# A transformer trunk layer on one Trainium2 core: all of x loaded first, and part of the modulation vector made by TensorE with the weight chunk stationary

## The reference, cut to what matters here

```python
c_act = silu(c)                                   # c: (1, 1024)
mod = c_act @ w_ada + b_ada                       # w_ada: (1024, 6144)
sh_m, sc_m, g_m, sh_f, sc_f, g_f = split(mod, 6)  # each 1024 wide
u = layer_norm(x) * (1 + sc_m) + sh_m             # x: (1024, 1024)
z = u @ w_in
...                                               # pooling, attention, convolution, merge, MLP
```

## Time and profile before

| | |
|---|---|
| runs | 1427.02, 1428.12, 1428.88 us; median 1428.12 |
| profiled execution, its own time | 1426.88 us |
| its span (first to last instruction) | 1425.1 us |
| PE busy | 1393.0 us (98%) |
| DVE busy | 969.4 us (68%) |
| ACT busy | 647.3 us (45%) |
| POOL busy | 421.8 us (30%) |
| mean granted TensorE clock | 0.993 |

### The profile page before, as it was taken

One profiled execution on the slowest core, in us unless ns is written; L12 is line 12 of the kernel. 1 busy time (PEld: TensorE's weight loads), 2 busy tenths in 40 slices (PEclk: granted clock), 3 DMA queues, 4 the chain that ended last, 5 costly groups with the idle time before them and its releaser, 6 DMA issues.

```text
span 1425.1 us, 17299 instructions
## 1 busy us (share of the span) xinstructions
PE 1393.0 (98%) x6522; PEld 1148.6 (81%) x6522; DVE 969.4 (68%) x1340; ACT 647.3 (45%) x914; POOL 421.8 (30%) x453
## 2 busy tenths in 40 slices
PE   7799999999999999999999999999999999999996
PEld 3688888888888888888888888888888888888885
DVE  5789677776479946464768797556565646437787
ACT  5522677777542124101616774443345535343251
POOL 1006465555566000000024327333444200001315
PEclk9899999999999999999999999999999999999998
DMA  9775465654565232762622555444445878456361
GB/s 347 266 266 159 148 185 156 188 168 149 161 234 172 89 104 79 245 192 86 200 114 89 183 181 193 142 145 146 156 163 207 297 277 299 162 211 236 118 222 60
DMA packets 159083, 256.42 MB, mean 180 GB/s; under 512 B 11352, under 2 KB 81422, under 8 KB 159000
## 3 DMA queue, kind: packets, MB, share of 16 engines
q1 hardware_dynamic: 144152, 204.97, 43.1%
q0 software_dynamic: 14848, 50.34, 10.5%
HBM read 182.36 MB, written 68.71 MB: 176 GB/s over the span
## 4 chain that ended last, share of the span: by engine, by line
PE 91%; DVE 5%; ACT 2%; issue 1%; DMA 1%; SPq 0%; DVEq 0%; ACTq 0%
PE ps L2065 24%; PE ps L2067 24%; PE ps L2066 24%; PE ps L2214 11%; PE ps L2254 2%; PE ps L2264 2%; PE ps L2279 2%; PE ps L2085 1%; DVE part_lo L1922 1%; PE ps L2129 1%; PE ps L2404 1%; DVE q L1983 0%; DMA k_raw<-tw_scratch 0%; DMA ada<-in_w_ada_dram 0%; DVE w_lo L1387 0%
## 5 line engine op out<-in xcount | busy, mean ns | idle before, releaser
L2065 PE MATMUL ps<-act_hi,w_hi 128*128 128x512 f32 (+1 forms) x480 | 187.2, 390 | 9.4 <-DVE act_lo L1482 9.4
L1922 DVE TENSOR_TENSOR part_lo<-k_raw,part_hi 128x1024 fp32r<-128x1024 f32 x112 | 146.1, 1332 | 58.6 <-ACT part_hi L935 55.4
L2067 PE MATMUL ps<-act_hi,w_lo 128*128 128x512 f32 (+1 forms) x480 | 184.6, 385 | 0.0
L2066 PE MATMUL ps<-act_lo,w_hi 128*128 128x512 f32 (+1 forms) x480 | 184.6, 385 | 0.0
L2065 PE MATMUL ps<-part_hi 128*128 128x512 f32 x448 | 174.3, 389 | 0.0
L2066 PE MATMUL ps<-part_lo,part_hi 128*128 128x512 f32 x448 | 174.3, 389 | 0.0
L2067 PE MATMUL ps<-part_hi,part_lo 128*128 128x512 f32 x448 | 174.3, 389 | 0.0
L935 ACT ACTIVATE part_hi<-k_raw 128x1024 fp32r<-128x1024 f32 x112 | 116.4, 1059 | 113.6 <-DMA k_raw<-tw_scratch 48.8
L2065 PEld LDWEIGHTS ps<-act_hi,w_hi 128*128 128x128 f32 x480 | 91.1, 190 | 28.4 <-issue 5.9
L1387 DVE TENSOR_TENSOR w_lo<-w_raw,w_hi 128x1024 fp32r<-128x1024 f32 x51 | 65.9, 1291 | 65.6 <-ACT w_hi L935 65.6
L2066 PEld LDWEIGHTS ps<-act_lo,w_hi 128*128 128x128 f32 x480 | 91.2, 190 | 18.4 <-issue 1.0
(11 more groups left out here) (260 smaller groups left out, 3202.4 us busy)
## 6 DMA issues: line engine op xcount, KB each, us to landing
k_raw<-h_scratch SPq DMA_DIRECT2D x112, 256.0 KB, 4.2
w_raw<-in_w_in_dram SPq DMA_DIRECT2D x42, 512.0 KB, 4.1
ada<-in_w_ada_dram SPq DMA_DIRECT2D x8, 2048.0 KB, 9.6
tw_rows<-in_w_ff_dram POOLq DMA_DIRECT2D x64, 256.0 KB, 4.1
tw_scratch<-tw_sum POOLq DMA_DIRECT2D x32, 512.0 KB, 3.7
h_scratch<-h_sum POOLq DMA_DIRECT2D x64, 256.0 KB, 3.0
k_raw<-tw_scratch SPq DMA_DIRECT2D x64, 256.0 KB, 5.4
pair_raw<-in_w_ff_dram SPq DMA_DIRECT2D x13, 1024.0 KB, 6.3
```

What stands on the lines that cost most here:

```text
L1922: nc.vector.tensor_tensor(part_lo[s][:, :, :], k_raw[rs][:, :, :], f(part_hi[s][:, :, :]), ALU.subtract)\
L2065: nc.tensor.matmul(out, sh, mh, start=first, stop=False)
L2066: nc.tensor.matmul(out, sh, ml, start=False, stop=False)
L2067: return nc.tensor.matmul(out, sl, mh, start=False, stop=last)
```

## The change

SP loads c, then all eight x tiles, then chunk 0, the small rows, chunk 2, weight blocks 0 and 1, chunk 1, weight block 2, chunk 3. Norm and transpose go tile by tile in place of pairs. Chunk 0, chunk 2 and the first half (k = 0 to 3) of chunk 3 are made by TensorE with the chunk stationary: for each of four groups of 128 columns and each k, one product whose stationary operand is 128x128 of the chunk and whose moving operand is one column of `c_act`. They give columns at once, so `save_ada_row` and `row_columns` go. The two halves of a sum lie in separate PSUM columns and are added by VectorE. VectorE makes chunk 1 whole and the second half of chunk 3.

```diff
@@ SP
             def load_ada(i):
-                if i == 3:
-                    sp.wait_ge(head_ps_done, 1)
+                if i in (3, 5):
+                    sp.wait_ge(reduced, DIRECT_ORDER.index(i - 3) + 1)
                 elif i == 4:
                     sp.wait_ge(partial_done, 1)
-                elif i == 5:
-                    sp.wait_ge(head_ps_done, 4)
                 elif i == 6:
-                    sp.wait_ge(partial_done, 2)
+                    sp.wait_ge(reduced, 4)
...
-            load_ada_half(0, 0)
-            load_x(range(2))
-            load_ada_half(0, 1)
-            load_x(range(2, 4))
+            load_x(range(ST))
+            load_ada(0)
...
-            load_ada_half(2, 0)
-            load_x(range(4, 6))
-            load_ada_half(2, 1)
-            load_x(range(6, ST))
+            load_ada(2)
             load_block(0)
+            load_block(1)
             load_ada(1)
-            load_block(1)
+            load_block(2)
             load_ada(3)
-            load_block(2)
@@ ACT
-            for i in range(0, ST, 2):
+            for i in range(ST):
                 take_root(i, i)
-                take_root(i + 1, i + 1)
-                norm(i, i, mid[:, i, :])
...
+                if i >= 1:
+                    norm(i - 1, i - 1, mid[:, i - 1, :])
+                if i >= 2:
+                    save_tile(i - 2)
+            cut_hi(0)
@@ DVE
+            for t in range(ST):
+                dve.wait_ge(x_in[t], 16)
+                stats(mid[:, t, :], t)
+                if t >= 1:
+                    scale_bias(t - 1, t - 1)
+            scale_bias(ST - 1, ST - 1)
...
             def start_chunk(i):
-                dve.wait_ge(ada_in[i % 3], 16 * (i // 3 + 1))
+                if i == 3:
+                    dve.wait_ge(ada_end_in[0], 32)
+                else:
+                    dve.wait_ge(ada_in[i % 3], 16 * (i // 3 + 1))
...
+                k0 = 4 if i == 3 else 0
...
             def mixer_columns(h):
...
-                link(nc.vector.tensor_tensor(out, total, bias, ALU.add))
+                link(nc.vector.tensor_tensor(out, low, bias, ALU.add))
                 scale = mod[:, KT + 4 * h:KT + 4 * h + 4]
+                if h == 0:
+                    link(nc.vector.tensor_tensor(out, high, out, ALU.add))
+                else:
+                    link(nc.vector.tensor_tensor(scale, ps[:, 7, 28:32], scale, ALU.add))
                 nc.vector.tensor_scalar_add(scale, scale, 1.0).then_inc(mod_done, 1)
...
+            for t in (ST - 2, ST - 1):
+                dve.wait_ge(z_done, t + 1)
+                dve.wait_ge(x_copied, ST - 2)
+                nc.vector.tensor_copy(x_t[:, :, t * P:(t + 1) * P], tile_banks(t)).then_inc(x_copied, 1)
...
             mixer_columns(0)
-            dve.wait_ge(z_done, ST)
-            nc.vector.tensor_copy(x_t[:, :, (ST - 1) * P:ST * P], tile_banks(ST - 1)).then_inc(x_copied, 1)
             cut_lo(0)
             cut_u_lo(0)
             cut_u_lo(1)
             cut_lo(1)
             cut_u_lo(2)
+            cut_u_lo(3)
             start_chunk(1)
-            cut_u_lo(3)
+            cut_lo(2)
             end_chunk(1)
-            cut_lo(2)
             ada_chunk(3)
             mixer_columns(1)
@@ PE
+            def direct_chunk(i, half):
+                pe.wait_ge((ada_in, ada_end_in)[half][i % 3], 16 * (i // 3 + 1))
+                if i == 3:
+                    pe.wait_ge(cols_done, 1)
+                for m in range(4):
+                    for k in range(4 * half, 4 * half + 4):
+                        col = 16 * half + 4 * i + m
+                        ins = nc.tensor.matmul(ps[:, 6 + i % 2, col:col + 1], ada[i % 3][:, k, m * P:(m + 1) * P],
+                                               c_act[:, k:k + 1], start=k % 4 == 0, stop=k % 4 == 3)
                 return ins
...
+            for i in range(6):
+                transpose_x(i)
             pe.wait_ge(head_sb_done, 2)
-            row_chunk(0, 0)
-            transpose_x(0)
-            transpose_x(1)
-            row_chunk(0, 1).then_inc(head_ps_done, 1)
-            transpose_x(2)
-            transpose_x(3)
+            direct_chunk(0, 0)
+            transpose_x(6)
+            direct_chunk(0, 1).then_inc(reduced, 1)
+            transpose_x(7)
...
-            row_chunk(2, 0)
-            transpose_x(4)
-            row_columns(0)
-            transpose_x(5)
-            row_chunk(2, 1).then_inc(head_ps_done, 1)
-            transpose_x(6)
-            row_columns(2)
-            transpose_x(7)
+            direct_chunk(2, 0)
+            direct_chunk(2, 1).then_inc(reduced, 1)
...
             for n in range(2):
                 for k in range(2, 4):
                     rows_part(n, k)
+            direct_chunk(3, 0)
             pe.wait_ge(w_lo_done, 3)
             for k in range(4):
                 rows_part(2, k)
-            row_columns(1)
-            row_columns(3)
+            reduce_first(1)
+            reduce_first(3)
```

More of the change, by code:

```diff
@@ L66 @@
 N_DIRECT = 2
-ROW_ORDER = (0, 2, 1, 3)
-ADA_BANKS = {0: 0, 2: 1}
+DIRECT_ORDER = (0, 2, 1, 3)
 P1_BANKS = (4, 2, 0, 6, 0, 2)
@@ L125, in trunk_layer @@
     h_pad = at("h_pad", [P, 2, PAD + SEQ], f32, X + 84 * KB)
-    ada_row = [h_pad[0:1, i // 2, PAD + i % 2 * HALF:PAD + (i % 2 + 1) * HALF] for i in range(4)]
     z_pool = mid[:, 0:2, :]
@@ L960, in _ @@
             nc.scalar.activation(c_sig[:, :], c_raw[:, :], ACT.Sigmoid).then_inc(head_sb_done, 1)
-            def save_ada_row(i):
-                act.wait_ge(head_ps_done, {0: 1, 2: 4}[i])
-                copy(ada_row[i], ps[0:1, ADA_BANKS[i], :]).then_inc(head_sb_done, 1)
             def save_tile(i):
@@ L1434, in start_chunk @@
                     dve.wait_ge(reduced, i - 3)
-                link(nc.vector.tensor_scalar(partial_of(i)[:, :], ada[i % 3][:, 0, :], c_act[:, 0:1], None, ALU.mult))
-                add_rows(i, range(1, 4))
+                k0 = 4 if i == 3 else 0
+                link(nc.vector.tensor_scalar(partial_of(i)[:, :], ada[i % 3][:, k0, :], c_act[:, k0:k0 + 1], None,
+                                             ALU.mult))
+                add_rows(i, range(k0 + 1, 4))
             def end_chunk(i):
-                if i in (1, 3):
-                    dve.wait_ge(ada_end_in[i % 3], 16 * (i // 3 + 1))
-                add_rows(i, range(4, 8))
+                if i == 1:
+                    dve.wait_ge(ada_end_in[1], 16)
+                add_rows(i, range(5 if i == 3 else 4, 8))
             def add_rows(i, ks):
@@ L1469, in mixer_columns @@
                 ks = slice(4 * h, 4 * h + 4)
-                out, total, bias = (t.rearrange("p (g k) -> p g k", g=2)[:, :, ks]
-                                    for t in (mod[:, 0:16], ps[:, 6 + h, 0:16], cols[:, 0:16]))
-                link(nc.vector.tensor_tensor(out, total, bias, ALU.add))
+                out, low, high, bias = (t.rearrange("p (g k) -> p g k", g=2)[:, :, ks] for t in (
+                    mod[:, 0:16], ps[:, 6 + h, 0:16], ps[:, 6 + h, 16:32], cols[:, 0:16]))
+                link(nc.vector.tensor_tensor(out, low, bias, ALU.add))
                 scale = mod[:, KT + 4 * h:KT + 4 * h + 4]
+                if h == 0:
+                    link(nc.vector.tensor_tensor(out, high, out, ALU.add))
+                else:
+                    link(nc.vector.tensor_tensor(scale, ps[:, 7, 28:32], scale, ALU.add))
                 nc.vector.tensor_scalar_add(scale, scale, 1.0).then_inc(mod_done, 1)
@@ L1483, in cut_u_lo @@
                     .then_inc(u_lo_done, 1)
+            for t in (ST - 2, ST - 1):
+                dve.wait_ge(z_done, t + 1)
+                dve.wait_ge(x_copied, ST - 2)
+                nc.vector.tensor_copy(x_t[:, :, t * P:(t + 1) * P], tile_banks(t)).then_inc(x_copied, 1)
+            dve.wait_ge(head_ps_done, 2)
+            nc.vector.tensor_copy(cols[:, 0:ROWS_A], ps[:, 7, PIECE:PIECE + ROWS_A])
+            nc.vector.tensor_copy(cols[:, ROWS_A:ROWS_A + ROWS_C], ps[:, 7, PIECE + P:PIECE + P + ROWS_C])\
+                .then_inc(cols_done, 1)
             mixer_columns(0)
-            dve.wait_ge(z_done, ST)
-            nc.vector.tensor_copy(x_t[:, :, (ST - 1) * P:ST * P], tile_banks(ST - 1)).then_inc(x_copied, 1)
             cut_lo(0)
@@ L2079, in _, with reduce_first @@
             pe.wait_ge(consts_done, 2)
[L2081 to L2086, removed]
-                return ins
[L2089 to L2095, removed]
-                for m in range(4):
[L2097 to L2101, removed]
+            def direct_chunk(i, half):
[7 more added lines that the diff above has]
+                                               c_act[:, k:k + 1], start=k % 4 == 0, stop=k % 4 == 3)
+                return ins
+            def reduce_first(i):
+                pe.wait_ge(partial_done, 1 + i // 2)
+                pe.wait_ge(cols_done, 1)
+                for m in range(4):
+                    col = (4 if i == 1 else 28) + m
```

(2 more changed lines are left out.)

## The result

The changed kernel takes 1446.0 us (median of four, 1445.01 to 1449.26) against 1428.1 before: ratio 1.013, 95% interval 1.0112 to 1.0147. The profiled execution took 1445.01 us with a span of 1443.2, so 18.1 more than the profiled one before. The median is inside the stated range (1432 to 1453), but 7.7 us above the forecast of 1438.3, and what fills those 7.7 us is the mechanism of rival A, in part.

What follows compares the result with a forecast made beforehand. TensorE (PE), busy 98% of the span, was taken as the bound, so head losses pass to the end: +7.2 + 3.4 - 0.6 + 0.2 = +10.2 us, forecast 1438.3 us; own range 1433 to 1442, stated range 1432 to 1453.

Steps and rivals of the forecast that it cites:

- rival A: Chunk products of stage one: PE stays at 1.2 GHz through all of them; sum +23.6 us, 1451.7 us; chance 0.2.
- The bound: Whole kernel: PE is busy 98% of the span; the head's gain or loss passes to the end one for one.
- Prices: One-column chunk products: 0.106 us a record, 3.4 us a half chunk, cost as before; small columns saved, 2.0 us.
- rival B: Chunk products: the weight loads hide under other products; put at -4 us, 1424 us; chance 0.07.
- Step 1: Head, x loaded first: ScalarE sets the pace, 2.4 us a tile; TensorE transposes tile 5 until 23.4 us.
- Step 3: Start of the chunk products: first 4 us at half speed, costing 2.1 us more; stage one ends at 42.2 us.
- sign of being wrong: Stretch of the chunk products: a clock of 0.50 throughout would show the forecast wrong.
- Steps 4 and 5: Modulation starts at 43.0 us, +7.2; stage two: half of chunk 3 +3.4, stall gone -0.6, third small operation +0.2.
- Step 6: SP's queue, block 2 ahead of chunk 3: DMAs idle some 9 us, slack 5 us or more, costs nothing.

## Why the prediction was right and where it was off

**The bound.** Right. What the head lost, +18.1 us by k = 4, is what the span lost.

**Prices.** Right at full clock: 0.107 us a record, 3.72 us for the first half chunk with its tail. The weight loads did not hide: rival B is out.

**Step 1.** ScalarE sets the pace, but 2.13 us a tile and not 2.4 (norms at 15.15, 17.32, 19.45), since its operations overlap by 0.1 each; and x tile 0 was there at 5.0, not 5.8. Tile 5 was done at 21.7 in place of 24.0, 2.3 us to the good.

**Step 3 failed.** "I take it to be still at 1.2 GHz when the chunk products begin [...] the first 4 us of products run at half speed." It was the other way round. By their lengths the transposes ran at full speed from 18.6 us on, the first half chunk too, and then the clock fell and stayed down to the end of the chunk products. The stretch from tile 5 to the last product of chunk 2 took 28.2 us and not 18.2: +10.0, less the 2.3 of step 1, is the 7.7 by which the forecast was short. The term was the clock's: 2.1 us in the forecast, 12.1 by the trace (28.2 less the 16.1 of the same work at full clock). Rival A had the cause right and was too high by 5.7 us (1451.7 for 1446.0), because tile 5 was done 2.3 us earlier and the first half chunk ran at full clock, 3.3. The sign of being wrong that the prediction gave, a clock of 0.50 throughout, came true in all but the first quarter of the products. The forecast's own range, 1433 to 1442, missed; the time lies in the stated range since that takes in A's value. Rival A had a chance of 0.2; the trace of before held no row against it but one stretch of a microsecond behind full products, and I should have given it about half. What I used against it, 59 to 60 us in the earlier trace rows, was too short a stretch and stood behind full products: the half chunk at 67.40, behind such products too, also ran at 1.00, and in four other profiles the clock fell just behind it.

**Steps 4 and 5.** Modulation starts 0.7 us after the last product (50.56), as worked out. Stage two grew by 3.1 us (2.8 expected: the half chunk 3.5, the stall at 48.86 gone, a longer stretch at half speed). VectorE ended chunk 3 at 70.5, six microseconds before TensorE took it, as said. The run with chunk 3 on VectorE gave back 2.9.

**Step 6.** Right: nothing, by the run that exchanges the two loads. The DMAs stood idle (0 GB/s from 36 to 49 us), for some 17 us and not 9, since the low part of block 0, which releases block 2, came 7.6 us later than forecast (51.7 for 44.1).

Of the 18 us, by the runs: undone alone, the one-column form of chunks 0 and 2 brings 8 to 9 and the half of chunk 3 on TensorE some 3. Undone together they bring 16.4 (1446.0 less 1429.6), so 4 to 5 us come only with both; 2 to 3 us are left for the loads, the pace and the order, the late start among them. Where the shared part lies: with both undone TensorE reaches the columns of chunk 1 18.5 us after its first product of block 0 (61.01 less 42.48), with the form alone undone after 23.5. The half of chunk 3 is 3.5 of that difference and the dip behind it about 1.5, which the profile of the changed kernel did not have; the half-speed stretches behind the gaps, which differ by 1 to 2 us between kernels, and the attention stage hold the rest. How these share it was not told apart.

## What to carry to other kernels

A matrix-vector product with the matrix stationary and one column moving cost about what the other form did while the clock was up (3.7 us a half chunk for 3.6), but a long row of them ran at half the clock (6.8), and so did the transposes between. Price such a row at both clocks, and if it must be, let more columns move: 64 equal ones cost nothing here and gave 9 us. They are no surety: one run of ten with them took 1445.58 us, at a lower clock. And before work is taken off one engine and put on another, ask which of the two ends last in that stage after the move: here 3.1 us off VectorE were worth nothing and 3.5 us on TensorE cost 2.9.

## What the runs showed of the hardware that I had not expected

TensorE's clock fell from 2.4 to 1.2 GHz while the engine was busy in every microsecond, under products of one moving column (clock 0.50 from 27 to 33 and 36 to 49 us), and stayed at 2.4 GHz under the same products with 64 columns moving (31 to 38 us). The Trainium skill (TensorE: Matmul & The Clock Gate, What's actually happening) lays the clock to how busy the engine has been; by the busy time the profile shows, this trace disagrees, and the measurement decides. A wide moving operand was free: at full clock a half chunk took 3.72 us with 1 column and 3.68 with 64. And filling a gap with unused products of 512 columns kept the clock up (first product 0.47 us long and not 0.77), with no gain that can be told, since another engine was the next to wait for.
